# One projection unit moved between the linear attention's state and output products, and the output units' weight halves split between the merges

## What is computed

```python
h = rmsnorm_2(x, norm1_g[l])
proj = h @ w_in[l]
q, k, v, r, a_low, u_pool, gate_gla, gate_pool = jnp.split(proj, split_idx, axis=-1)
...
inc = jnp.einsum('bhnsd,bhnsv->bhndv', k_end, vc)          # what each chunk adds to the state
def step(state, inp):
    dec, u = inp
    return dec[..., None] * state + u, state
...
o = o_intra + jnp.einsum('bhntd,bhndv->bhntv', q_dec, s_prev)
...
o = (head_rmsnorm(o, gla_norm_g[l]) * jax.nn.silu(r.astype(jnp.float32))).astype(x.dtype)
y_gla = o @ w_gla_branch[l]
y_pool = pool_mix(u_pool, pool_w[l], pool_scale[l]) @ w_pool_branch[l]
merged = jax.nn.sigmoid(gate_gla) * y_gla + jax.nn.sigmoid(gate_pool) * y_pool
x = x + merged @ w_out[l]
```

## Time and profile before

| | us |
|---|---|
| median of 3 runs | 862.65 |
| lowest and highest of them | 862.65, 929.07 |
| the profiled execution, its device time | 863.23 |
| the span of its trace | 861.5 |

### The profile page before, as it was taken

How to read it: one execution, slowest core, us unless ns; L and a number is a source line. 1 busy time by engine, 2 the same in 40 slices (tenths; PEclk the granted TensorE clock), 3 DMA queues, 4 the chain that set the end, 5 groups by cost and what they waited for, 6 DMA issues and landing times.

```text
span 861.5 us, 13151 instructions
## 1 busy us (share of the span) xinstructions
PE 813.7 (94%) x4792; PEld 661.8 (77%) x4792; DVE 523.9 (61%) x658; ACT 452.6 (53%) x592; POOL 126.5 (15%) x94
## 2 busy tenths in 40 slices
PE   6999999999999996998999989879999999999994
PEld 4888755999999995597899986566767676767672
DVE  3244326456566655555055493857887878787874
ACT  2243444454445443545155343357777777777763
POOL 0000001222432343102000000011111111111110
PEclk9999999999999998999699999889999999999998
DMA  9922222454555553143054554048999999999971
GB/s 363 396 99 88 89 87 79 148 186 175 180 192 195 189 172 126 49 147 147 5 192 151 192 196 146 1 147 309 367 359 371 355 363 371 359 363 370 363 288 50
DMA packets 25090, 181.44 MB, mean 211 GB/s; under 512 B 2784, under 2 KB 3040, under 8 KB 3296
## 3 DMA queue, kind: packets, MB, share of 16 engines
q1 hardware_dynamic: 25056, 180.97, 56.7%
HBM read 179.91 MB, written 1.05 MB: 210 GB/s over the span
## 4 chain that ended last, share of the span: by engine, by line
PE 87%; DVE 6%; ACT 3%; POOL 2%; issue 1%; DMA 1%; POOLq 0%; ACTq 0%; SPq 0%; DVEq 0%
PE psum L827 37%; PE psum L1036 15%; PE psum L1051 12%; PE psum L523 4%; PE psum L622 3%; PE psum L1057 3%; PE psum L531 2%; PE psum L581 1%; ACT junk L1167 1%; PE psum L1043 1%; PE psum L1028 1%; PE psum L946 1%; DVE arena L1794 1%; DVE ffn_w_low L441 1%; PE psum L944 1%
## 5 line engine op out<-in xcount | busy, mean ns | idle before, releaser
L441 DVE TENSOR_TENSOR ffn_w_low<-ring,ffn_w_high 128x2048 fp32r<-128x2048 f32 x57 | 135.1, 2373 | 123.5 <-ACT ffn_w_high L436 123.5
L436 ACT ACTIVATE ffn_w_high<-ring 128x2048 fp32r<-128x2048 f32 x57 | 109.2, 1918 | 144.3 <-PE psum L827 144.1
L827 PE MATMUL psum<-ht_high,ffn_w_high 128*128 128x256 f32 x576 | 164.4, 285 | 1.7 <-DVE ffn_w_low L441 1.1
L827 PE MATMUL psum<-ht_low,ffn_w_high 128*128 128x256 f32 x576 | 163.6, 284 | 0.0
L827 PE MATMUL psum<-ht_high,ffn_w_low 128*128 128x256 f32 x576 | 163.6, 284 | 0.0
L441 DVE TENSOR_TENSOR expert_w_low<-ring,expert_w_high 128x2048 fp32r<-128x2048 f32 x48 | 110.0, 2292 | 20.5 <-ACT expert_w_high L436 19.8
L827 PEld LDWEIGHTS psum<-ht_high,ffn_w_high 128*128 128x128 f32 x576 | 111.2, 193 | 3.2 <-issue 1.4
L827 PEld LDWEIGHTS psum<-ht_low,ffn_w_high 128*128 128x128 f32 x576 | 111.2, 193 | 0.3
L1051 PE MATMUL psum<-ring,arena 128*128 128x512 f32 x248 | 111.4, 592 | 0.0
L1036 PE MATMUL psum<-expert_w_high,xw 128*128 128x256 f32 x384 | 105.9, 311 | 5.8 <-POOL xw L1573 3.9
L827 PEld LDWEIGHTS psum<-ht_high,ffn_w_low 128*128 128x128 f32 x576 | 111.2, 193 | 0.0
(11 more groups left out here) (304 smaller groups left out, 1418.1 us busy)
## 6 DMA issues: line engine op xcount, KB each, us to landing
ring<-units_in SPq DMA_DIRECT2D x165, 1024.0 KB, 6.6
rows<-rows_in SPq DMA_DIRECT2D x1, 1688.0 KB, 12.7
arena<-bias_in SPq DMA_DIRECT2D x1, 1536.0 KB, 15.8
small<-small_in SPq DMA_DIRECT2D x1, 1232.0 KB, 25.6
const<-const_in SPq DMA_DIRECT2D x1, 1073.0 KB, 23.2
X<-x_in SPq DMA_DIRECT2D x1, 1024.0 KB, 4.9
out<-HN SPq DMA_DIRECT2D x2, 512.0 KB, 3.0
vec<-vec_in SPq DMA_DIRECT2D x1, 113.5 KB, 4.5
```

Of the source, the lines that this page charges most:

```text
L436: nc.scalar.activation(parts_slot(n)[0], w, ACT.Copy).then_inc(hi_ready, 1)
L441: nc.vector.tensor_tensor(l, ring[:, n % RING, :], h.bitcast(fp32), SUB).then_inc(lo_ready, 1)
L827: last = mm(o, l[a], r[b], start=start and (a, b) == pairs[0], stop=stop and (a, b) == pairs[-1])
```

## The change

Unit 6 moves on PE from behind the output products to the place between the state products and the output products. ACT's `split_hi` and DVE's `split_lo` of unit 8, which need unit 6's slot, move ahead of the squares and of the roots. In the output stage ACT makes the high half of W1 directly after that of W0, ahead of the third and fourth copies of merged tokens, and that of W2 behind these copies; DVE makes the low half of W1 between `merge(1, 0)` and `merge(1, 1)`. No instruction is added or removed.

```diff
--- before.py
+++ after.py
@@ -932,6 +932,9 @@
                               V[base:base + HD, n // 2, f * S:(f + 1) * S], start=True, stop=True)
                 last.then_inc(inc_done, 1)
 
+            pe.wait_ge(pool_in, 2)
+            gla_unit(6, 6)
+
             pe.wait_ge(st_sb, 2)
             pe.wait_ge(states_ready, 3)
             for odd in range(2):
@@ -947,8 +950,6 @@
                                       SS[base:base + HD, n - 1, f, odd * P:(odd + 1) * P],
                                       start=False, stop=n == chunks[-1])
                 last.then_inc(o_done, 1)
-            pe.wait_ge(pool_in, 2)
-            gla_unit(6, 6)
             gla_unit(7, 7)
             for j in range(4):
                 gla_unit(8 + j, (2, 3, 0, 5)[j])
@@ -1373,10 +1374,12 @@
                 copy(UP[:, 2 * j:2 * j + 2, PAD:PAD + S], proj_bank(6 + j)).then_inc(pool_in, 1)
             act.wait_ge(kend_tr, 1)
             copy(KET, proj_bank(0)).then_inc(kend_sb, 1)
+            split_hi(act, U_GLA + 8)
             act.wait_ge(o_done, 2)
             mean_squares(9, [psum[:, b, n * P:(n + 1) * P] for b in (1, 4) for n in range(4)])
             for j in range(2):
-                split_hi(act, U_GLA + 8 + j)
+                if j == 1:
+                    split_hi(act, U_GLA + 9)
                 act.wait_ge(unit_used, U_GLA + 7 + j)
                 nc.scalar.activation(RS[:, 2 * j:2 * j + 2, :], proj_bank(6 + j), ACT.Silu).then_inc(g_act, 1)
             for dst, first in ((SG, 8), (SP, 12)):
@@ -1397,8 +1400,10 @@
             for j in range(4):
                 act.wait_ge(merged, j + 1)
                 copy(HTH[:, 2 * j:2 * j + 2, :], HT[:, 2 * j:2 * j + 2, :]).then_inc(merged_hi, 1)
-                if j >= 1:
-                    split_hi(act, U_WOUT2 + j - 1)
+                if j == 1:
+                    split_hi(act, U_WOUT2)
+                    split_hi(act, U_WOUT2 + 1)
+            split_hi(act, U_WOUT2 + 2)
             split_hi(act, U_WOUT2 + 3)
             act.wait_ge(unit_used, U_EXP - 1)
             split_hi(act, U_EXP)
@@ -1869,6 +1874,7 @@
                         last = stt(SS[:, n, f, :], SS[:, n - 1, f, :], DEC[:, f, n:n + 1], inc, MUL, ADD)
                 last.then_inc(states_ready, 1)
                 dve.wait_ge(states_ready, n + 1)
+            split_lo(dve, U_GLA + 8)
             add_eps(9)
             roots_ready(9)
             for odd in range(2):
@@ -1879,7 +1885,6 @@
                                  rstd[:, 9, at:at + 2].unsqueeze(2).to_broadcast([P, 2, P]), MUL)
                 last.then_inc(ohn_ready, 1)
 
-            split_lo(dve, U_GLA + 8)
             split_lo(dve, U_GLA + 9)
             dve.wait_ge(pool_sums, 1)
             for g, w in enumerate(POOL_WINDOWS):
@@ -1929,10 +1934,11 @@
             merged_low(1)
             split_lo(dve, U_WOUT2)
             merge(1, 0)
+            split_lo(dve, U_WOUT2 + 1)
             merge(1, 1)
             merged_low(2)
             merged_low(3)
-            for n in range(1, 4):
+            for n in range(2, 4):
                 split_lo(dve, U_WOUT2 + n)
             split_lo(dve, U_EXP)
             dve.wait_ge(unit_used, U_EXP)
```

## The result

The changed kernel takes 851.0 us (median of four runs, 849.99 to 852.74); the kernel before, on the same chip, 863.19 (median of four). The ratio is 0.9863, with a 95% interval of 0.9839 to 0.9887; one of the four executions before took 929.07 us, in the slow state, and is not in the ratio (the median of the other three is 862.65). That is 1.4% faster, within the 2% that the chances were stated for, and inside the range of 845.5 to 855.0. The profiled execution took 852.74 us and has a span of 850.8, against 863.23 and 861.5.

The account below looks back on a forecast made before the run. PE's list, with its waits and clock, was taken to bound the kernel. Unit 7's 11.3 us plus the output stage's 2.3 made 13.6 off the profiled 863.23 (849.6; 849.05 from the median), stated as 849.3, range 845.5 to 855.0.

Parts of the forecast that it names:

- What bounds the kernel: Whole kernel: the time PE's list takes, waits and clock included; the chain runs through PE for 87% of the span.
- Rival C: Nothing is gained, since the transfers bound the stage: 863 us; chance 0.03.
- Start of unit 6 and its 5.76 us: Behind the state products: unit 6 starts at 405.1, takes 5.76 us at the full clock and ends at 410.9.
- The output products, 6.8 us: Behind unit 6: 4.28 us of records plus 2.5 for 16 row changes, in place of 13.26; bounds 5.9 and 9.0.
- Rival E: Output products: row changes cost 0.29 us each at full clock too, 4.7 in place of 2.5, so 851.5; chance 0.05.
- Unit 7 11.3 us earlier: Unit 7 starts at 417.7, not 428.98: 3.26 idle, 6.5 from the output products, 1.6 from unit 6.
- ACT, DVE and SP at nothing: Around the output products: unit 8's and 9's halves, the squares and the loads delay nothing, cost zero.
- Part 2: Output stage, reordered weight halves: W1 does not wait, W2 waits some 0.45 us; gain 2.3 us, bounds 1.0 and 2.76.
- The sum: Whole kernel: 11.3 + 2.3 = 13.6 us less, giving 849.3 us.
- rival B: Router and later stages: only places of low clock shift, about 1.6 us each, 846.1 to 852.5; chance 0.14.
- Rival A: The clock falls within the output products: 854.3 us if in the middle, 857.4 if at their start; chance 0.20.
- D: Slower: low clock from the output products holds through dense units, 4.5 us more each, 883 with six; chance 0.02.

Follow-up runs that it names:

- fillers in the gap: The kernel before plus four unused 512-column products between the state and output products, no unit moved: 855.62 us, ratio 0.9927.
- part 1 alone: The kernel before with unit 6 between state and output products, unit 8's halves ahead of the squares, output stage unchanged: 851.84 us, ratio 0.9885.
- part 1 on PE only: The kernel before with unit 6 moved ahead of the output products on PE, unit 8's halves in their old places: 854.11 us, ratio 0.9923.

## Why the prediction was right, point by point

**What bounds the kernel.** PE's list, its waits and its clock: confirmed by the fillers in the gap, which added work and made the kernel 0.7% faster. Rival C, the transfers, is out: their share from 429 to 460 is 0.47 with units 10.6 us earlier.

**Start of unit 6 and its 5.76 us.** Put at 405.1, it came at 404.77 in an execution that was 0.28 ahead. With the change of rows at its start it takes 5.85 us (404.77 to 410.62). The forecast holds.

**The output products, 6.8 us.** They took 7.46. This is the term that was mis-sized. The clock was 1.00, as forecast; the 16 changes of rows cost 3.2 us, 0.20 each in the mean, and not 2.5. The two figures from rows 5, 0.10 and 0.21, were read rightly but put down to the wrong changes. One half of a change stands between the groups and the other half behind the first record that follows. The first step, directly behind unit 6, has no change ahead of it and is 0.32 us (410.62 to 410.94), 0.11 more than its two records, as in rows 5; all later steps of one product are 0.41 to 0.42, in both directions. The second half of a change back to 128 rows shows in what follows it: unit 7 takes 5.85 us where unit 8 takes 5.76, and in the first block, in the kernel before, eight records of L531 take 1.99 us behind 64 rows and 1.89 behind 128:

```profile
65.09 1.89 PE L531 MATMUL psum<-ring,HT 128*128 128x256 f32 x8
```

So the 0.10 of rows 5 was half a change, and the 0.21 the second half of that one and the first half of the next. Rival E had 0.29 us each at either clock, and with it 9.0 us; the measured mean of 0.20 lies between. The Trainium skill says that the drain takes nearly the same wall time at either clock (TensorE: Matmul & The Clock Gate, Single matmul latency). This cost does not follow that rule: it is 0.29 us at the low clock and 0.20 at the full one, a ratio of 1.4.

**Unit 7 11.3 us earlier.** It was 10.62 net of the earlier start; the difference is the 0.66 us of the products. The clock's share is 7.3 us of it (5.80 in the products, 1.49 in unit 6), the rest the idle time.

**ACT, DVE and SP at nothing.** Right for the change as it was made: unit 8's high half at 410.88, its low half at 412.90, and no wait for it. Wrong was the side remark that the halves would be in time in their old place too: that costs 1.99 us. I had counted the squares and not DVE's scaling behind them.

**Part 2, 2.3 us.** Measured 2.09 alone and 2.24 with part 1. W1 does not wait, and W2 starts 11.38 us behind W0, where the forecast had 11.37 (506.53 to 517.9); its wait is 0.23 and not 0.45, since W0 and W1 themselves took 0.25 us longer than I had put.

**The sum.** 13.6 us were forecast and 12.77 came, up to the end of W3. Of these 2.4 did not reach the end, since more of the router's and the first expert's work stood at the low clock. That is rival B, at 0.14, with its price (852.5 as its upper end, against 852.74 of this execution and 851.0 in the median). So the forecast's mechanism was right, two thirds of a microsecond of its size were wrong, and a rival came true behind it; 863.23 less the 12.77 us alone would have been 850.5. What of the executions' spread is rival B alone can't be told from these runs, since only profiled executions show where the clock fell.

**Rival A,** the low clock in the output products, at 0.20, did not come, nor did D: the clock is 1.00 from 402.8 to 425, in all traces with unit 6 or fillers in the gap. The Trainium skill's case of a clock that swings under many short idles (the same page, A second HAM failure mode: psum-queue depth-cycling) did not come out in the output products, with 16 changes of rows in 7.46 us. Among the router's products, where PE is busy too, the clock did fall (4.26 us in place of 3.73).

## What to carry to other kernels

A wait of PE is worth more than its length if the clock falls behind it: here 3.26 us of idle cost 10.6, and independent work in the gap, unit 6 or four useless products, brought the clock's part back. When a step of PE is moved, follow its consumers too: the halves of the unit two places on were late by 2 us until ACT and DVE were moved along. Small plain products of mixed row counts should be grouped by rows, and those of 64 rows taken by turns from the two row halves: the same twenty products went from 7.46 to 3.42 us.

## What the runs showed of the hardware that I had not expected

A change between 128 and 64 rows costs 0.20 us in both directions at the full clock, half of it behind the first record that follows, and 0.29 at the low one. Products of 64 rows from the two row halves, by turns, overlap in full: 24 records in 1.61 us, where one half takes 1.60 for 12. An idle time of 2.49 us ahead of W1 passed without consequence in two kernels (before, part 1 alone) and was followed by 3.4 us at the clock 0.50 in two others (fillers in the gap, part 1 on PE only). Moving the router and the first expert by 1.7 us changed their length by as much the other way. For a kernel like this a gain of 2 us upstream is not safe until the traces of the stages behind it have been read.
